# Block two's attention with the values as the stationary operand, two heads in the array's column halves, and the probabilities scaled before they are transposed

## The reference

```python
h = modulate_2(rmsnorm_2(x, mix_norm[l]), sh2, sc2)
z = h @ w_in[l]
q_lat, kv_lat, k_pe_raw, ca_q, ca_k, ca_v, gate_a, gate_b = jnp.split(z, splits, axis=-1)
y_a = mla_attention(q_lat, kv_lat, k_pe_raw, positions, ...) @ w_branch_a[l]
y_b = chunk_attention(ca_q.reshape(shp), ca_k.reshape(shp), ca_v.reshape(shp),
                      rel_bias[l]) @ w_branch_b[l]
merged = jax.nn.sigmoid(gate_a) * y_a + jax.nn.sigmoid(gate_b) * y_b
x = x + g2[:, None, :] * (merged @ w_out[l])
```

```python
s = jnp.where(mask[None, None], s, NEG_INF)
p = jax.nn.softmax(s, axis=-1).astype(v.dtype)
return jnp.einsum('bhqk,bkhd->bqhd', p, v)
```

## Time and profile before

| | before |
|---|---|
| three runs | 1200.26, 1195.83, 1199.83 us (median 1199.83) |
| profiled execution | 1195.08 us, span 1193.2 us |
| mean granted TensorE clock | 0.973 |
| TensorE, VectorE, ScalarE, GpSimd busy | 95%, 70%, 48%, 27% |
| slots 0 to 15 of the attention | 856 to 932 us |
| branch products, out product | 932 to 958, 959 to 989 us |

### The profile page before, as it was taken

How to read it: one execution, slowest core, us unless ns; L and a number is a source line. 1 busy time by engine, 2 the same in 40 slices (tenths; PEclk the granted TensorE clock), 3 DMA queues, 4 the chain that set the end, 5 groups by cost and what they waited for, 6 DMA issues and landing times.

```text
span 1193.2 us, 19118 instructions
## 1 busy us (share of the span) xinstructions
PE 1131.8 (95%) x7764; PEld 1026.6 (86%) x7764; DVE 834.4 (70%) x960; ACT 569.5 (48%) x729; POOL 319.6 (27%) x274
## 2 busy tenths in 40 slices
PE   2998999899999899999899999999999989999996
PEld 2998988899999788888788888889998989888885
DVE  1578556695568487777878777779665796755676
ACT  3494433444444444444454544455655525444442
POOL 4000657775675300000100000020456761000000
PEclk8899999999999899999999999989999988999998
DMA  9924554577866487778648777737764654665670
GB/s 290 290 91 142 176 178 148 180 238 242 262 219 225 146 281 250 245 247 296 212 145 273 255 260 246 234 127 250 237 202 145 214 172 159 211 200 187 221 255 36
DMA packets 192547, 250.28 MB, mean 210 GB/s; under 512 B 4859, under 2 KB 171966, under 8 KB 192350
## 3 DMA queue, kind: packets, MB, share of 16 engines
q1 hardware_dynamic: 183838, 216.92, 56.0%
q0 software_dynamic: 8640, 32.38, 8.1%
HBM read 248.23 MB, written 1.05 MB: 209 GB/s over the span
## 4 chain that ended last, share of the span: by engine, by line
PE 57%; POOL 15%; DVE 11%; DMA 10%; ACT 3%; issue 2%; SPq 2%; POOLq 0%; DVEq 0%; ACTq 0%
PE twin L1297 55%; DMA ada_raw<-in_w_ada 9%; POOL ada_raw L781 7%; POOL ada_raw L786 4%; DVE wlo L1903 3%; DVE arena L1903 3%; DVE arena L1911 2%; POOL ada_raw L789 2%; ACT arena L873 2%; POOL arena L790 1%; PE twin L1358 1%; DMA arena<-in_w_ada 1%; ACT whi L873 1%; DVE X L1903 1%; PE twin L1623 0%
## 5 line engine op out<-in xcount | busy, mean ns | idle before, releaser
L1297 PE MATMUL twin<-A_both,whi 128*128 128x256 f32 (+1 forms) x2208 | 580.6, 340 | 5.3 <-DVE X L1903 4.2
L1903 DVE TENSOR_TENSOR wlo<-raw,whi 128x2048 fp32r<-128x2048 f32 x169 | 409.0, 2421 | 139.3 <-ACT whi L873 139.2
L1297 PE MATMUL twin<-A_both,wlo 128*128 128x256 f32 x1632 | 437.1, 281 | 0.0
L873 ACT ACTIVATE whi<-raw 128x2048 fp32r<-128x2048 f32 x169 | 323.2, 1913 | 206.9 <-PE twin L1297 206.4
L1297 PEld LDWEIGHTS twin<-A_both,whi 128*128 128x128 f32 x2208 | 371.5, 190 | 47.8 <-issue 10.2
L1297 PEld LDWEIGHTS twin<-A_both,wlo 128*128 128x128 f32 x1632 | 310.0, 190 | 11.1 <-DVE A_both L1903 0.2
L781 POOL TENSOR_TENSOR ada_raw<-ada_raw,arena 128x512 f32<-128x512 f32 (+1 forms) x64 | 111.8, 1771 | 126.2 <-DMA ada_raw<-in_w_ada 126.2
L873 ACT ACTIVATE arena<-twin 128x512 f32<-128x512 f32 (+5 forms) x167 | 88.4, 555 | 114.6 <-PE twin L1297 84.8
L873 ACT ACTIVATE arena<-arena 128x512 f32<-128x512 f32 (+7 forms) x132 | 69.8, 558 | 149.2 <-DVE arena L1903 116.5
L1297 PE MATMUL twin<-whi,A_both 128*128 128x256 f32 x640 | 120.6, 290 | 8.5 <-DVE A_both L1903 4.8
L1297 PE MATMUL twin<-whi,B_hi 128*128 128x512 f32 (+2 forms) x340 | 126.6, 372 | 0.2 <-DVE B_lo L1903 0.2
(11 more groups left out here) (134 smaller groups left out, 1178.0 us busy)
## 6 DMA issues: line engine op xcount, KB each, us to landing
raw<-in_w_in SPq DMA_DIRECT2D x48, 1024.0 KB, 5.6
raw<-in_ffn_w_in SPq DMA_DIRECT2D x44, 1024.0 KB, 5.1
ada_raw<-in_w_ada POOLq DMA_DIRECT2D x28, 1024.0 KB, 6.3
ada_raw<-in_w_ada SPq DMA_DIRECT2D x24, 1024.0 KB, 5.4
raw<-in_w_ffn_in SPq DMA_DIRECT2D x22, 1024.0 KB, 5.2
raw<-in_ffn_w_out SPq DMA_DIRECT2D x22, 1024.0 KB, 5.0
raw<-in_w_ffn_out SPq DMA_DIRECT2D x11, 1024.0 KB, 5.0
arena<-in_w_ada SPq DMA_DIRECT2D x8, 1024.0 KB, 11.8
```

The lines of the kernel that those rows point to most:

```text
L873: return nc.scalar.activation(o, i, f, **kw)
L1297: return nc.tensor.matmul(o, l, r, start=start, stop=stop, **kw)
L1903: return nc.vector.tensor_tensor(o, x, y, op)
```

## The change

- The value product is turned round: the values of one head and key tile (128 keys by 64 features) are the stationary operand and occupy 64 of the array's 128 columns, the transposed probabilities (128 queries) move. Heads h and h+4 write to the lower and the upper 64 partitions of the same bank, in turns. The result stands with features on the partitions and tokens along the row, as the branch products need it. For that the pairs of heads of tile 1 become (0,4), (1,5), (2,6), (3,7).
- The row's reciprocal can no longer be applied to the output, whose partitions aren't tokens. VectorE applies it to the probabilities of job s-1 in slot s (`scale_rows`), in SBUF, ahead of the transposes, which now wait for it.
- `heads_out`, `out_group` and their buffers go. The merges to high and low parts read the value banks directly, in slots 7, 9, 13 and 15.
- The features now lie in another order (head h in one half, h+4 in the other), so the branch weights' rows are loaded in that order: four loads of 1 MB become eight of half of it, each to 64 partitions.
- The scores of jobs 9 and 11 go to other banks, and the columns that keep the row sums are numbered by the place in the job.

```diff
@@ -103,7 +103,7 @@
     JOBS += [(_kind, 0, (0, 2, 4, 6)), (_kind, 0, (1, 3, 5, 7))]
-    JOBS += [(_kind, 1, hs) for hs in ((0, 2), (1, 3), (4, 6), (5, 7))]
+    JOBS += [(_kind, 1, hs) for hs in ((0, 4), (1, 5), (2, 6), (3, 7))]
 NJ = len(JOBS)
@@ -122,6 +122,10 @@
 ADA_POOL = [n for n in range(len(ADA)) if n not in ADA_DVE]
+
+MERGE_SLOT = {7: (0, 0), 9: (0, 1), 13: (1, 0), 15: (1, 1)}
+
+HALVED = [BASE_P2 + n for n, (kind, _) in enumerate(P2) if kind in ("bra", "brb")]
@@ -434,7 +435,8 @@
-            return lin(16, i, 16 * (u // RING + 1))
+            more = sum(1 for v in HALVED if v <= u and v % RING == u % RING)
+            return lin(16, i, 16 * (u // RING + 1 + more))
@@ -488,7 +490,7 @@
             w = a["w_branch_a_2"][0] if kind == "bra" else a["w_branch_b_2"][0]
-            return cview(w, 512 * n, 512), 4, 512
+            return w.rearrange("(i k p) n -> i p k n", i=2, p=VD)[:, :, :, 512 * n:512 * n + 512], 4, 512
@@ -509,6 +511,10 @@
                 dst = dd_w if kind == "dd" else raw[ring(u)][:, 0:k * w].rearrange("p (k w) -> p k w", k=k)
+                if u in HALVED:
+                    for i in range(2):
+                        sp.dma_start(dst[VD * i:VD * i + VD], src[i]).then_inc(landed[ring(u)], 16)
+                    return
                 sp.dma_start(dst, src).then_inc(landed[ring(u)], 16)
@@ -654,7 +660,13 @@
-            return 3 if j % 2 and j < NJ - 2 else 6
+            return 6 if j % 2 == 0 else 3 if j < 8 else 0
+
+        def job_row(j):
+
+            kind, t, heads = JOBS[j]
+            n = 4 * (j % 6) if t == 0 else 2 * (j % 6 - 2)
+            return 2 * (kind == "ca") + t, n
@@ -1206,11 +1218,11 @@
                             act.wait_ge(jx_done, j + 1)
-                            row = 2 * (kind == "ca") + t
-                            for x, h in enumerate(heads):
+                            row, n0 = job_row(j)
+                            for x in range(len(heads)):
                                 v = Pb[j % 2][:, K * x:K * x + K]
                                 ins = run(v, v, ACT.Exp, bias=mx[:, j % 2, x:x + 1], scale=-1.0,
-                                          accum_out=sm[:, row, h:h + 1])
+                                          accum_out=sm[:, row, n0 + x:n0 + x + 1])
                             ins.then_inc(jp_done, 1)
@@ -1218,26 +1230,21 @@
                             run(pT[j % 2], bank[7][:]).then_inc(jt_sb, 1)
-                        if slot in (13, 14):
-                            merge_high(0, slot - 13)
+                        if slot in MERGE_SLOT:
+                            merge_high(*MERGE_SLOT[slot])
                     if P2[n2] in (("bra", 0), ("bra", 1)):
...
                         run(v, v, ACT.Sigmoid).then_inc(gates_done, 1)
-                    if P2[n2] == ("bra", 1):
-                        merge_high(1, 0)
-                        merge_high(1, 1)
                 partial_squares(5)
...
-                g = 2 * kk + m
-                act.wait_ge(ot_tr, g + 1)
+                act.wait_ge(jo_mm, 6 * kk + 2 * m + 4)
                 k = 4 * kk + 2 * m
-                b = bank[6] if kk == 0 else bank[m]
-                run(B_hi[:, k:k + 2, :], b[:].rearrange("p (m t) -> p m t", m=2)).then_inc(ohi_done, 1)
+                run(B_hi[:, k:k + 2, :], bank[2 * kk + m][:].rearrange("p (m t) -> p m t", m=2)).then_inc(ohi_done, 1)
@@ -1605,7 +1612,9 @@
-                            pe.wait_ge(js_sb, slot if slot == NJ - 1 else slot - 1)
+                            pe.wait_ge(js_sb, slot - 1)
+                        if slot == 9:
+                            pe.wait_ge(olo_done, 1)
                         for x, h in enumerate(heads):
@@ -1616,7 +1625,7 @@
                         j = slot - 2
-                        pe.wait_ge(jp_done, j + 1)
+                        pe.wait_ge(pn_done, j + 1)
                         if j:
@@ -1626,29 +1635,17 @@
                         pe.wait_ge(jt_sb, j + 1)
-                        o = bank[t + 2 * (kind == "ca")]
                         v = vm if kind == "mla" else cav
-                        for x, h in enumerate(heads):
-                            for kt in range(t + 1):
-                                c = P * (x * (t + 1) + kt)
-                                ins = mm(o[:, VD * h:VD * h + VD], pT[j % 2][:, c:c + P], v[:, kt, VD * h:VD * h + VD],
-                                         kt == 0, kt == t)
+                        nh = len(heads)
+                        for kt in range(t + 1):
+                            for x in sorted(range(nh), key=lambda x: heads[x] % 4):
+                                h = heads[x]
+                                i, k = divmod(h, 4)
+                                o = bank[k // 2 + 2 * (kind == "ca")]
+                                c, f = P * (x * (t + 1) + kt), T * (k % 2) + P * t
+                                ins = mm(o[VD * i:VD * i + VD, f:f + P], v[:, kt, VD * h:VD * h + VD],
+                                         pT[j % 2][:, c:c + P], kt == 0, kt == t, skip_group_check=True)
                         ins.then_inc(jo_mm, 1)
-
-                def out_group(kk, m):
-
-                    pe.wait_ge(osb_done, kk + 1)
-                    b = bank[6] if kk == 0 else bank[m]
-                    if kk == 0 and m == 0:
-                        pe.wait_ge(js_sb, NJ)
-                    if kk == 0 and m == 1:
-                        pe.wait_ge(olo_done, 1)
-                    o = osb if kk == 0 else osb2
-                    for x in range(2):
-                        for t in range(TT):
-                            f0 = P * (2 * m + x)
-                            ins = nc.tensor.transpose(b[:, T * x + P * t:T * x + P * t + P], o[:, t, f0:f0 + P], ident)
-                    ins.then_inc(ot_tr, 1)
@@ -1701,15 +1698,12 @@
                                 ins.then_inc(half_out, 1)
-                            after_half(n2, half, job, out_group)
+                            after_half(n2, half, job)
                     if kind == "ukv":
-                        after_half(n2, 0, job, out_group)
-                        after_half(n2, 1, job, out_group)
-                    if (kind, n) == ("bra", 1):
-                        out_group(1, 0)
-                        out_group(1, 1)
-
-            def after_half(n2, half, job, out_group):
+                        after_half(n2, 0, job)
+                        after_half(n2, 1, job)
+
+            def after_half(n2, half, job):
                 if n2 == 3 and half == 0:
@@ -1746,8 +1740,6 @@
                     job(slot)
-                    if slot in (13, 14):
-                        out_group(0, slot - 13)
@@ -2440,7 +2432,7 @@
                         bias = U.rearrange("p (k h) -> p h k", h=H2)
-                        bias = bias[:, heads[0]:heads[0] + 2 * nh - 1:2, 0:K][:, :, ::-1]
+                        bias = bias[:, heads[0]:heads[-1] + 1:heads[1] - heads[0], 0:K][:, :, ::-1]
                         ins = stt(s3, b3, -(float(VD) ** -0.5), bias, ALU.mult, ALU.subtract)
@@ -2448,23 +2440,20 @@
-                def heads_out(kk, o):
-
-                    dve.wait_ge(jo_mm, 6 * kk + 6)
-                    for t in range(TT):
-                        ins = nc.vector.reciprocal(rin[:, 2 * kk + t, :], sm[:, 2 * kk + t, :])
-                    link(ins)
-                    for t in range(TT):
-                        ins = tt(o[:, t, :].rearrange("p (h d) -> p h d", h=H2),
-                                 bank[2 * kk + t][:].rearrange("p (h d) -> p h d", h=H2),
-                                 rin[:, 2 * kk + t, :].unsqueeze(2).to_broadcast([P, H2, VD]), ALU.mult)
-                    ins.then_inc(osb_done, 1)
+                def scale_rows(j):
+
+                    row, n0 = job_row(j)
+                    nh = len(JOBS[j][2])
+                    r = rin[:, row, n0:n0 + nh]
+                    s3 = Pb[j % 2].rearrange("p (h k) -> p h k", h=nh)
+                    dve.wait_ge(jp_done, j + 1)
+                    link(nc.vector.reciprocal(r, sm[:, row, n0:n0 + nh]))
+                    tt(s3, s3, r.unsqueeze(2).to_broadcast([P, nh, 512 // nh]), ALU.mult).then_inc(pn_done, 1)
...
                     k = slice(4 * kk + 2 * m, 4 * kk + 2 * m + 2)
-                    b = bank[6] if kk == 0 else bank[m]
                     dve.wait_ge(ohi_done, 2 * kk + m + 1)
-                    rest(B_lo[:, k, :], b[:].rearrange("p (m t) -> p m t", m=2), B_hi[:, k, :]).then_inc(olo_done, 1)
+                    rest(B_lo[:, k, :], bank[2 * kk + m][:].rearrange("p (m t) -> p m t", m=2), B_hi[:, k, :]).then_inc(olo_done, 1)
@@ -2487,17 +2476,12 @@
                             job(slot)
+                        if slot is not None and 1 <= slot <= NJ:
+                            scale_rows(slot - 1)
                         if slot is not None and half == 0:
                             split(BASE_P2 + n2 + 2)
-                        if slot == 10:
```

(10 more changed lines are left out.)

5 lines of the change are left out of this document (1 added, 4 removed).

## The result

Over ten runs of each on one chip the changed kernel took 1200.81 us (median), the kernel before 1196.84; the ratio is 1.0033, 95% interval 1.0019 to 1.0047. The profiled execution of the changed kernel took 1202.65 us (span 1200.8), that of before 1195.08 (span 1193.2). I forecast no difference, with a gain of TensorE that GpSimd takes back. That mechanism was there, but the change cost 4 us net.

A forecast was written before the change was run, and what follows sets the result against it. TensorE, busy 95% of the span, was taken as the bound, with GpSimd 3.08 us behind it. TensorE alone came 8 us early at the last norm, but GpSimd's later end left +0.2 us: 1199.5 us, range 1193 to 1206.

The forecast's parts named there:

- The end of the sum: Last norm's shift and scale products: start at 989.5 against 989.30, +0.2 us, and nothing differs between the kernels behind it.
- slot 12: Before slot 12's transposes: TensorE stands about 4.7 us, job 11 coming 1.5 us later; bounds 0 and 8 us.
- the first branch product: Sum at the first branch product behind the attention: -2.5 - 0.7 + 3.3 = +0.1 us, the same time.
- GpSimd's end: End of GpSimd's unit 47, needed by the last norm: 989.5 instead of 986.2, 3.3 us later.
- six scalings: About six of VectorE's 12 scalings fall into GpSimd operations, which wait 0.7 us each, 4.2 us.
- the half loads: Branch weight loads halved: landing, even doubled to 10.2 us, is covered by 15.2 us before first read; costs nothing.
- Values as stationary operand: Attention's 12 value-product jobs: 0.60 instead of 0.81 us each, 2.5 us off TensorE; bounds 4.1 off, 1.6 more.
- no transposes between the branch products: Eight transposes behind the second branch product go with their wait for copies and subtractions, 2.2 us off.
- the out product's wait: TensorE's wait before the block's output product shrinks from 4.79 to about 1.5 us, with the low clock behind it.
- a wait of the norm's products: Before the last norm's products TensorE, alone ready at 981, waits several us until GpSimd releases it.
- Rival A: The forecast itself: GpSimd takes the place of TensorE's gain, -3 to +3 us, 1196.5 to 1202.5; chance 0.52.
- Rival C: VectorE overflows in slots 6 to 12, its scalings and splits delayed by locks: +6 to +8 us, 1206 to 1208; chance 0.16.

The follow-up runs named there:

- b_m9: Kernel before, with modulation unit 40 reduced by VectorE instead of GpSimd, at step 9 of the plan (1, 3, 5, 7, 9): 0.9968, 1192.70 us.
- b_m9_2: Kernel before, with unit 40 moved from GpSimd to VectorE at step 9, the same kernel run again beside the changed kernel with that move: 0.9958.

## Why the prediction was wrong

- **The end of the sum failed: "Behind it both kernels do the same."** I had TensorE waiting there for GpSimd, and priced the wait and nothing behind it. The granted clock was 0.50 from the wait's end on, and the norm's products took 6.85 instead of 4.18 us. Of the 3.46 us lost up to the first product behind the norm, 1.29 are the later start (forecast +0.2), 2.17 lie behind it (forecast 0). The row that should have warned me was my own, where 0.50 followed the 4.79 us wait of before; I used it for the output product and not here.
- **The same in slot 12.** I forecast a wait of 4.7 us, by a split put off behind a scaling, which is what the trace has. I got 2.75, but at half the clock its half product took 5.92 us (924.53 to 930.45) instead of 3.76 (918.64 to 922.40 before), 2.2 more. At the first branch product TensorE was 2.8 us late (+78.5 against +75.7), not level; ready for the norm's products it was at +130.8, where I had it at +124.6 (981).
- **GpSimd's end: +4.3 us, forecast +3.3, by the wrong cause.** I counted six scalings that fall into GpSimd's operations and cost it 0.7 us each. In the trace three of the 12 were stretched (to 2.28, 1.88 and 1.18 us), and GpSimd's operations took 0.8 us more in all; its last seven waits for loads took 43.6 us against 38.3. I had put the half loads at nothing, since their reader has cover, and had not asked what stands behind them on GpSimd's queue: 2.5 us of it is the load behind the halves (7.50 against 5.03). The rest is one load issued 0.9 us behind a whole one (8.14 against 5.21), and which ones meet so closely depends on where the splits fall. Against that, unit 40 began 1.8 us earlier from slot 0. The waits were as long in the kernel that had its scaling on ScalarE (43.7, end at +135.4). How much of this the change moved stays open: b_m9 and b_m9_2, one program, ended at +115.8 and +125.3, and taking the half loads out changed no time.
- **Values as stationary operand: the records as forecast, the job not.** The eight take 907.04 - 906.45 = 0.59 us (forecast 0.60). But the transposes before them grew from 0.49 (906.93 to 907.42) to 0.58, so a slot went from 5.41 (900.46 to 905.87 before) to 5.30 us (899.51 to 904.81), 0.11 less instead of 0.21; over 12 jobs 1.3 us instead of 2.5. The Trainium skill, page "TensorEngine Tiling (Array Packing)", section Key Properties, has TensorE drain at a change of tiling mode; these rows fit it. I had allowed 0.13 us for both changes; the row before alone grew by 0.09.
- **Right:** no transposes between the branch products, the out product's wait down from 4.79 to 2.33 us (forecast 1.5), and a wait of the norm's products released by GpSimd. Rival A had its name and place. Rival C (the slots overflow) was set against it as an alternative, at 1206; the runs show half of it present at once: the scalings cost TensorE some 5 us (ready at +130.8 against +125.8, one execution each), hidden behind GpSimd's end only in part. I let two costs share one place and took the larger, where both counted: GpSimd's wait comes with a clock of its own, and its phase differs from run to run. That the median, 1200.81, lies near the forecast of 1199.5 is luck in part: the kernel before came out 3 us below the median of three runs that I had forecast from.

## What to carry to other kernels

When a change puts another engine's end in front of TensorE, price the clock behind the wait as well as the wait: here 2.2 us behind each of the changed kernel's two waits (2.75 and 3.33 us), as against the kernel before. A SBUF-to-SBUF tensor_tensor on VectorE is not a 0.7 us operation where GpSimd works; in a chain that TensorE waits for, try it on ScalarE. When a load is cut in two, look at the loads behind it on every queue, and not only at its own reader. And try the same relief on the kernel before: the best complete form of the changed kernel, 0.9963, gains no more than the old kernel does with the same unit moved off GpSimd (0.9968 and 0.9958).

## What the runs showed that I had not expected

- Moving one unit of 10 us off an engine that bounded nothing gained 0.3 to 0.4% (b_m9, b_m9_2). In one trace its turns fell less on VectorE's last chain, in the other they did not, so the way it gains is not shown.
- The same program's executions differ by 3 us in where TensorE stands at the norm (+128.3 in b_m9, +131.7 in b_m9_2) and by 9.5 us in GpSimd's end, so a trace of one execution can't carry a claim of less than that; the ratios can.
- A pair of half loads took longer to land than one whole load of twice the size, and held up GpSimd's load behind it by some 2.5 us.
